# The second layer's memory keys computed in three reduced products instead of one full float32 product

## The chip, the cores and the metric

The kernel runs on one core of one Trainium2 chip. The metric is the device time of one launch in microseconds (us). Names used below: PE is the matrix engine (TensorE), ACT is ScalarE, DVE is VectorE, POOL is GpSimd, SP is the engine that issues most of the weight loads. PSUM is the memory that PE accumulates into.

## The reference, cut to what matters

The whole network is two blocks of two layers each, about 3.1 ms of work; the change touches one product in the second layer of the first block. There the layer norm of the memory, `mem_n` (256 tokens by 1024), is the same for both layers, and each layer makes its own keys and values of it.

```python
def memory_attention(q, mem_n, w_kv):
    k, v = jnp.split(mem_n @ w_kv, 2, axis=-1)      # 256 x 1024 each
    ...
    s = einsum(qh, kh) * (XA_HEAD_DIM ** -0.5)
    o = einsum(softmax(s), vh)

# second layer (i = 1)
u, z, xq = split_cols(h @ w_in, [2048, 3072, 1024])
seq_out = s5(u)                                      # a scan over the 512 tokens
xa = memory_attention(xq, mem_n, xa_w_kv[1])
x = x + (concat([seq_out, xa]) * silu(z)) @ w_out[1]
```

`mem_n @ w_kv[:, :1024]` of this layer is the product that the change is about.

## The kernel before, in words

All activations are held feature-major: 128 features on the partitions, tokens along the free axis. The weights of the whole network are one stream of units of 128 by 1024 float32 (512 KB). SP loads unit after unit into `ring`, which has 4 slots. SP loads unit u when unit u-3 has begun, which the semaphore `begun` counts: PE adds one to it with the first matmul of each unit (for one range of tokens).

A `Gemm` stage multiplies by such a stream. Kind "fm": one output tile of 128 features by all tokens per unit here (8 inner tiles of 128, `KD`). It comes in two forms.

- Plain (`high` is None): PE reads `ring` as float32, one `mm` for each inner tile (line 271). The profile shows two matmul records for each of them.
- In three products (`high` given): weights and activations are each written as a high part rounded to the type fp32r and a low part, the rest. ACT makes the high part of a unit into one of the two slots of `high` (`make_high`, line 363), POOL subtracts it from the unit into `ring_r` (`make_low`, line 354), and PE adds three products: high by high (line 261), high weights by low activations (line 264), low weights by high activations (line 266). Before the first product of a unit PE waits for its low part (`unit_lo`, in `unit`). ACT makes the high part of unit u only when `begun` has reached u, that is when unit u-1 has begun, as there are two slots.

Nearly all large products of the kernel have the second form. `mem_k1`, the memory's keys of the second layer, has the plain one: 8 outputs, 8 units, 256 tokens (`MEMS`), stored by ACT and DVE in turn (`BOTH`, lines 3186 and 3189).

The order of the stages around it is written by hand and is the same on each engine:

1. `u`, the product for the scan's input, 16 outputs. It runs inside the stage `S5Inputs`, which also does, three outputs later (`LAG`), the scan's input blocks 0 to 12: 8 small matmuls each (line 1600) whose tables of 512 KB POOL loads (`load_next`, line 1572). There are two buffers for the tables, so table n+2 is loaded when block n is done (semaphore `added`).
2. `mem_k1`.
3. `S5LastInputs`: blocks 13, 14 and 15, and on POOL the loads of tables 14 and 15.
4. `S5Scan`: 63 steps on DVE alone. It starts when all blocks are copied out.
5. During the scan PE does `xq1`, `z1_xa` (three products each, 512 tokens) and `mem_v1` (plain, 256 tokens).
6. `xa1`, the attention, which waits for the scan and for `mem_v1`. Its scores are line 896.

The numbers of blocks and tables run from 0 to 15. `memn` is the normed memory, 128 by 8 by 256. `z_lo` and `z_hi` are the split parts of another activation; their tiles are free between the first layer's last product (`out0`) and a later stage. `b.norms["parts"]`, `out_hi` and `out_lo` count activations' high and low parts.

Of the kernel before, what the change touches and what calls it, by code (L numbers as in the profile page):

```python
# [16 lines left out]
ALU = mybir.AluOpType  # L17
ACT = mybir.ActivationFunctionType
# [7 lines left out]
KD = D // P  # L26
# [19 lines left out]
MEMS = [(0, N_MEM)]  # L46
# [4 lines left out]
class Chain:  # L51


    def __init__(self, eng, sem):
        self.eng, self.sem, self.n = eng, sem, 0
# [29 lines left out]
class Stage:  # L85
# [5 lines left out]
    def scalar(self, act):  # L91
        pass

    def vector(self, dve):
        pass

    def gpsimd(self, pool):
        pass


class Gemm(Stage):
# [13 lines left out]
    def __init__(self, b, name, kind, x, kt, outs, ranges, store, engines, needs, tiles=None, before=None,  # L115
                 high=None, x_hi=None, after=None, ready=None, slots=None, first_bank=0, late=None):
        self.ready = ready
        self.first_bank = first_bank
        self.after_banks = None
        self.fed = False  # L120
        self.squared_by = None
        self.beside = False
        self.low_elsewhere = False
        self.stored_elsewhere = False
        self.between = None
        self.first_use = {}
        self.flip = 0
        self.late, plain = late, int(late is not None)
        self.then = self.follows = None
        self.after = after  # L130
        self.b, self.name, self.kind, self.x, self.kt = b, name, kind, x, kt
        self.ranges, self.store, self.engines, self.needs = ranges, store, engines, needs
        self.tiles, self.before = tiles, before
        if kind == "fm":
            self.per_out = kt // 8
            self.slots = slots or (4 if len(ranges) == 1 else 2)
            self.body_outs = self.slots
            while self.body_outs * self.per_out % RING:
                self.body_outs += self.slots
            if outs < self.body_outs or outs % self.body_outs:  # L140
                self.body_outs = outs
            self.body_units = self.body_outs * self.per_out
            self.iters = outs // self.body_outs
            self.pars = [o % 2 for o in range(self.body_outs)]
        else:
            self.body_units = kt // 2
            self.body_outs = len(tiles)
            self.tile_banks = list(range(len(tiles)))
            self.slots = len(tiles)
            self.iters = outs  # L150
            self.pars = [i % 2 for i in range(len(tiles))]
        self.unit0 = b.units
        self.full0 = list(b.full)
        self.body_par = [self.pars.count(0), self.pars.count(1)]
        self.peel = min(self.full0) == 0 or self.iters == 1 or before is not None or high is not None
        self.high, self.x_hi, self.split0 = high, x_hi, b.splits - plain
        if high is not None:
            assert self.body_units % 2 == 0 or self.iters == 1, name
            b.splits += self.body_units * self.iters - plain
        b.units += self.body_units * self.iters  # L160
        b.full = [f + self.iters * n for f, n in zip(b.full, self.body_par)]
        self.done = list(b.full)
        if self.iters > 1:
            assert self.body_units % RING == 0, name
# [287 lines left out]
    def gpsimd(self, pool):  # L452
        if self.high is None or self.beside or self.low_elsewhere:
            return

        def body(it):
            for j in range(self.body_units):
                if not (self.late and isinstance(it, int) and it + j == 0):
                    self.make_low(pool, j, it)
        self.loop(pool, body)  # L460

# [794 lines left out]
NB = S5_G // 8  # L1256
# [289 lines left out]
class S5Inputs(Stage):  # L1546
# [7 lines left out]
    def __init__(self, b, m, beside, needs):  # L1554
        self.b, self.m, self.beside, self.needs = b, m, beside, needs
        beside.beside = True
        self.u_in = [b.sem("s5i_u_even"), b.sem("s5i_u_odd")]
        self.block_in = [b.sem("s5i_in_even"), b.sem("s5i_in_odd")]
        self.added = b.sem("s5i_added")
        self.x_kept = b.sem("s5i_x_kept")  # L1560
        self.done = (self.x_kept, NB)

    def load_rows(self, sp, n):

        for k in range(S5_C):
            sp.dma_start(self.m.u[16 * (7 - k):16 * (7 - k) + 16, n * 8:n * 8 + 8],
                         self.b.d_u[n * P:(n + 1) * P].rearrange("(g h) t -> h g t", h=S5_H)[:, :, S5_J * k:S5_J * (k + 1)]
                         ).then_inc(self.u_in[n % 2], 16)
# [5 lines left out]
    def gpsimd(self, pool):  # L1574
        gemm = self.beside
        for s, v in self.needs:
            pool.wait_ge(s, v)
        self.load_table(pool, 0)
        self.load_table(pool, 1)
        gemm.low_unit(pool, 0)  # L1580
        for n in range(NB):
            gemm.low_unit(pool, n + 1)
            if n > self.LAG:
                self.load_next(pool, n - self.LAG - 1)

    def load_next(self, pool, n):

        pool.wait_ge(self.added, n + 1)
        if n + 2 < NB:
            self.load_table(pool, n + 2)  # L1590
# [19 lines left out]
    def scalar(self, act):  # L1610
        gemm = self.beside
        if not gemm.fed:
            gemm.high_unit(act, 0)
        for n in range(NB):
            gemm.high_unit(act, n + 1)
            gemm.out_scalar(act, n)

    def block_vector(self, dve, n):

        b, m = self.b, self.m  # L1620
        dve.wait_ge(self.added, n + 1)
        to = m.state[:, n, 1:S5_J, :]
        b.nc.vector.tensor_copy(to, b.ps[:, 4 + n % 2, :].rearrange("p (g j) -> p j g", g=8)[:, 0:S5_J - 1, :]
                                ).then_inc(self.x_kept, 1)

    def vector(self, dve):
        self.b.chain.link(self.b.nc.vector.memset(self.m.state[:, :, 0, :], 0.0))
        for n in range(NB - self.LAG):
            self.block_vector(dve, n)


class S5LastInputs(Stage):
# [1466 lines left out]
def build(nc, a, out):  # L3099

    with ExitStack() as ctx:
        b = Board(nc, ctx)
# [81 lines left out]
        def copy(which, to, ps, scale=None):  # L3184
            if which == "act":
                return nc.scalar.activation(to, ps, ACT.Copy, scale=1.0 if scale is None else scale)  # L3186
            if scale is not None:
                return nc.vector.tensor_scalar(to, ps, scale, None, ALU.mult)
            return nc.vector.tensor_copy(to, ps)

        def keep(to, scale=None):
            return lambda which, m, parts, o: copy(which, to[:, m, :], parts[0], scale)

        BOTH, A, V = ("act", "dve"), ("act", "act"), ("dve", "dve")
        stages = []
# [60 lines left out]
        memn = lambda k: b.memn[:, k, :]  # L3256
# [3 lines left out]
        def tm_keep(to, width=512):  # L3260
            return lambda which, m, part, o: copy(
                which, to[0:part.shape[0], m[1], bass.ds(m[0] * width, width)], part)
# [29 lines left out]
        class StoreMemory(Stage):  # L3292


            def __init__(self, needs):
                self.needs = needs
# [44 lines left out]
        def add_x(which, m, parts, o):  # L3341
# [15 lines left out]
        s5r = S5Responses(b, m5, g, [gla.done] + tables.done, done(gz0))  # L3357
# [3 lines left out]
        high = b.high  # L3361
        out0_done = [(b.stored[0], g.done[0]), (b.stored[1], g.done[1])]
# [5 lines left out]
                  hi=lambda k: chunked(h_hi(k)[:, 0:L1]), lo=lambda k: chunked(h1_lo(k)), added=True)  # L3368
# [5 lines left out]
        def send_u(act, m, o, par, n):  # L3374
# [7 lines left out]
                           high=high, x_hi=h_hi, after=send_u))  # L3382
        rms.feed(stages[-1])
        gu = stages[-1]
        km1, vm1, xq1 = view(30848, KD, N_MEM), view(28800, 2, D), view(20480, 8, L1)
# [9 lines left out]
        m5.ustage = [memf[:, i * 512:(i + 1) * 512] for i in range(2)]  # L3395
        s5i = S5Inputs(b, m5, gu, tables.done + out0_done)
        stages.append(s5i)
        stages.append(Gemm(b, "mem_k1", "fm", memn, KD, KD, MEMS, keep(km1), BOTH, s5r.done))
        stages.append(S5LastInputs(s5i))
        scan = S5Scan(b, m5, [s5i.done])  # L3400
        stages.append(scan)
# [1 line left out]
        stages.append(Gemm(b, "z1_xa", "fm", h1_lo, KD, D // P, FULL,  # L3403
                           lambda which, m, parts, o: nc.scalar.activation(b.z[:, m + 16, :], parts[0], ACT.Silu), A, [],
                           high=high, x_hi=h_hi))
        stages[-2].lead(stages[-1])
        stages.append(Gemm(b, "mem_v1", "tm", memn, KD, 2, None, tm_keep(vm1), A, [], MEM_TILES))
        g = stages[-1]
# [6 lines left out]
                  high=high, x_hi=h_hi)  # L3415
# [12 lines left out]
                   high=high, x_hi=m5.y_hi)  # L3428
# [15 lines left out]
        def add_x1(which, m, parts, o):  # L3444
# [6 lines left out]
                           x_hi=z_hi, ready=split_z.ready))  # L3451
# [365 lines left out]
```

## Time and profile before

| what | value |
|---|---|
| median of 3 runs | 3115.97 us (3114.11 to 3116.03) |
| the profiled execution | 3121.37 us |
| its span (first to last instruction) | 3119.6 us |
| mean clock granted to PE in it | 0.965 of full |
| PE busy | 2871.5 us (92%) |
| POOL busy | 1067.7 us (34%) |
| ACT busy | 986.1 us (32%) |

Busy shares are means over stages with different limits. The span lacks what lies around the instructions, 1.8 us here. A name such as `arena` is one large buffer that holds many tensors in turn, so a row is placed by its line and time. In the rows "PEclk" is the clock granted to PE, 1.00 for 2.4 GHz and 0.50 for 1.2 GHz. A bracket as [1.10 <-POOL ring_r L354] is the idle time of the engine before this row and what ended it.

### The profile page before, as it was taken

What the parts mean: (1) busy time and instruction counts of PE and PEld (TensorE: products, weight loads), DVE (VectorE), ACT (ScalarE), POOL (GpSimd) and SP (SyncE); (2) the same over time, 40 slices, a digit from 0 to 9 for tenths busy, and PEclk for the clock granted to TensorE, in tenths of its full rate; (3) what the DMA queues carried; (4) which work ended last, traced back from release to release, by engine and by line L of the source; (5) the groups of instructions that cost most, each with busy time, mean ns of one, the idle gap of its engine ahead of it and who ended that gap; (6) DMA issues with size and microseconds to landing.
All of it is one profiled execution on the core that took longest, in us unless ns stands there. A gap on an engine that the chain in (4) does not pass through costs nothing.

```text
span 3119.6 us, 44776 instructions
## 1 busy us (share of the span) xinstructions
PE 2871.5 (92%) x17854; PEld 2346.1 (75%) x17854; DVE 1397.9 (45%) x2227; ACT 986.1 (32%) x1505; POOL 1067.7 (34%) x749
## 2 busy tenths in 40 slices
PE   6988989899899999998989888899998999899997
PEld 4666567677688578786778876799998866668885
DVE  5788364600206611302138574470634345293452
ACT  3222354222312236423225332312124454332221
POOL 0233122344324179444433410144442321234442
PEclk9999999999999999999999998999999998899999
DMA  3898111244572279322222100122222210122222
GB/s 134 260 259 268 69 41 48 78 135 161 154 211 98 95 182 262 104 95 74 88 86 68 36 3 22 61 94 89 88 94 74 78 42 20 54 81 94 95 94 74
DMA packets 130750, 324.85 MB, mean 104 GB/s; under 512 B 54145, under 2 KB 54785, under 8 KB 129809
## 3 DMA queue, kind: packets, MB, share of 16 engines
q1 hardware_dynamic: 96128, 221.90, 21.8%
q0 software_dynamic: 30096, 88.21, 10.2%
q10 hardware_dynamic: 4352, 12.26, 1.0%
q8 instruction: 130, 2.13, 0.3%
q14 instruction: 44, 0.35, 0.0%
HBM read 288.32 MB, written 33.95 MB: 103 GB/s over the span
## 4 chain that ended last, share of the span: by engine, by line
PE 69%; DVE 18%; DMA 4%; ACT 3%; issue 3%; POOL 3%; DVEq 1%; ACTq 0%; SPq 0%; POOLq 0%
PE ps L261 16%; PE ps L264 16%; PE ps L266 16%; PE ps L271 3%; DMA d_pb<-arena 3%; POOL ring_r L354 2%; DVE h L593 1%; PE ps L2829 1%; PE ps L915 1%; PE ps L1769 1%; PE ps L573 1%; PE ps L1510 1%; PE ps L1600 1%; PE ps L2180 1%; PE ps L2804 1%
## 5 line engine op out<-in xcount | busy, mean ns | idle before, releaser
L354 POOL TENSOR_TENSOR ring_r<-ring,high 128x1024 fp32r<-128x1024 f32 x327 | 815.5, 2494 | 1449.9 <-ACT high L363 1449.8
L261 PE MATMUL ps<-h_hi,high 128*128 128x512 f32 (+1 forms) x2104 | 735.1, 358 | 40.3 <-DVE ring_r L354 13.1
L266 PE MATMUL ps<-h_hi,ring_r 128*128 128x512 f32 (+1 forms) x2104 | 661.6, 349 | 0.0
L264 PE MATMUL ps<-h_r,high 128*128 128x512 f32 (+1 forms) x1912 | 643.1, 346 | 0.0
L363 ACT ACTIVATE high<-ring 128x1024 fp32r<-128x1024 f32 x359 | 379.5, 1057 | 822.8 <-PE ps L261 697.4
L261 PEld LDWEIGHTS ps<-h_hi,high 128*128 128x128 f32 x2104 | 399.6, 190 | 117.2 <-issue 48.9
L266 PEld LDWEIGHTS ps<-h_hi,ring_r 128*128 128x128 f32 x2104 | 369.8, 190 | 53.5
L264 PEld LDWEIGHTS ps<-h_r,high 128*128 128x128 f32 x1912 | 364.5, 191 | 41.6 <-issue 1.4
L264 PE MATMUL ps<-f_r,high 128*128 128x264 f32 (+1 forms) x832 | 261.2, 326 | 0.0
L261 PE MATMUL ps<-f_hi,high 128*128 128x264 f32 (+1 forms) x768 | 236.6, 321 | 0.0
L261 PE MATMUL ps<-z_hi,high 128*128 128x512 f32 x488 | 197.9, 405 | 29.7 <-POOL ring_r L354 23.9
L266 PE MATMUL ps<-f_hi,ring_r 128*128 128x264 f32 (+1 forms) x768 | 205.0, 321 | 0.0
L266 PE MATMUL ps<-z_hi,ring_r 128*128 128x512 f32 x488 | 193.2, 396 | 0.0
L264 PEld LDWEIGHTS ps<-f_r,high 128*128 128x128 f32 x832 | 156.7, 188 | 14.4
L3186 ACT ACTIVATE arena<-ps 128x512 f32<-128x512 f32 (+4 forms) x102 | 58.4, 576 | 339.2 <-PE ps L266 250.1
L261 PEld LDWEIGHTS ps<-f_hi,high 128*128 128x128 f32 x768 | 144.4, 188 | 11.4
L264 PE MATMUL ps<-z_lo,high 128*128 128x512 f32 x360 | 145.7, 405 | 0.0
L261 PEld LDWEIGHTS ps<-z_hi,high 128*128 128x128 f32 x488 | 93.4, 191 | 59.6 <-POOL ring_r L354 21.6
L266 PEld LDWEIGHTS ps<-f_hi,ring_r 128*128 128x128 f32 x768 | 127.0, 188 | 11.0
L3619 DVE CAST f_hi<-f x64 | 131.6, 2056 | 7.8
L264 PE MATMUL ps<-z_hi,high 128*128 128x512 f32 x280 | 112.1, 400 | 0.0
L266 PEld LDWEIGHTS ps<-z_hi,ring_r 128*128 128x128 f32 x488 | 93.5, 192 | 22.5
(465 smaller groups left out, 4271.1 us busy)
## 6 DMA issues: line engine op xcount, KB each, us to landing
ring<-in_units SPq DMA_DIRECT2D x402, 512.0 KB, 3.2
d_ca<-arena POOLq DMA_DIRECT2D x16, 640.0 KB, 9.3
arena<-d_ca POOLq DMA_DIRECT2D x16, 640.0 KB, 5.7
arena<-d_q POOLq DMA_DIRECT2D x32, 256.0 KB, 8.3
d_pb<-arena POOLq DMA_DIRECT2D x16, 512.0 KB, 11.4
arena<-d_pb POOLq DMA_DIRECT2D x16, 512.0 KB, 4.1
arena<-d_ca POOLq DMA_DIRECT2D x16, 512.0 KB, 5.0
arena<-d_k POOLq DMA_DIRECT2D x128, 64.0 KB, 4.2
```

Of the source, the lines that this page charges most:

```text
L261: part = mm(acc, hi[:, cols], self.x_hi(k)[:, t0:t0 + tn], start=(k == 0), stop=False)
L264: mm(acc, hi[:, cols], self.x(k)[:, t0:t0 + tn], start=False, stop=False)
L266: ins = mm(acc, w[:, cols], self.x_hi(k)[:, t0:t0 + tn], start=False, stop=(k == self.kt - 1))
L271: ins = mm(acc, w[:, k % 8 * P:(k % 8 + 1) * P], self.x(k)[:, t0:t0 + tn], start=(k == 0), stop=(k == self.kt - 1))
L354: eng.tensor_tensor(b.ring_r[:, slot, :], b.ring[:, slot, :], self.high[:, (j + self.flip) % 2, :], ALU.subtract).then_inc(b.unit_lo, 1)
L363: b.nc.scalar.activation(self.high[:, (j + self.flip) % 2, :], b.ring[:, u % RING, :], ACT.Copy).then_inc(b.unit_hi, 1)
L573: ins = b.nc.tensor.matmul(b.ps[:, bank, 0:tn], b.ones[:, :], b.sq[:, k % 2, t0:t0 + tn], start=(k == 0), stop=(k == self.n - 1))
L593: b.nc.vector.scalar_tensor_tensor(out=self.out(k), in0=self.view(self.x(k)), scalar=self.w(k), in1=self.view(b.inv[:, 0:self.tokens]), op ...
L915: ins = b.nc.tensor.matmul(b.ps[:, 6 + c, :], self.v[:, m, (2 * h + c) * P:(2 * h + c + 1) * P], self.pt[:, h % 2, m, :], start=(m == 0), ...
L1510: ins = mm(b.ps[0:S5_H, 4 + 2 * par + g // 4, g % 4 * P:(g % 4 + 1) * P], m.ca[par][:, g, 144:160], m.ca[par][:, g, 0:P], start=True, stop ...
L3186: return nc.scalar.activation(to, ps, ACT.Copy, scale=1.0 if scale is None else scale)
L3619: nc.vector.tensor_copy(hi, t).then_inc(mlp_parts, 1)
```

## The change

`mem_k1` is given the form in three products. Its activation, the normed memory, is split during the u product by a new class `SplitMemory`, in four quarters of 128 by 512: ACT makes the high parts after outputs 3 to 6 of `u`, POOL the low parts during outputs 4 to 7. They lie in free tiles of `z_lo` (high parts) and `z_hi` (low parts). The first weight unit of `mem_k1` is split ahead, at the end of `S5Inputs` (`follower`); its other seven are split as those of other products are. The first weight unit of `xq1` is split by ACT just before the last store of `mem_k1` (`lead`).

```diff
@@ class Gemm
+        self.low_given = False
@@ Gemm.gpsimd
             for j in range(self.body_units):
-                if not (self.late and isinstance(it, int) and it + j == 0):
+                if not ((self.late or self.low_given) and isinstance(it, int) and it + j == 0):
                     self.make_low(pool, j, it)
@@ S5Inputs.gpsimd
         gemm.low_unit(pool, 0)
         for n in range(NB):
             gemm.low_unit(pool, n + 1)
+            if 4 <= n < 8:
+                self.memory.low(pool, n - 4)
             if n > self.LAG:
                 self.load_next(pool, n - self.LAG - 1)
+        self.follower.low_unit(pool, 0)
@@ S5Inputs.scalar
         for n in range(NB):
             gemm.high_unit(act, n + 1)
+            if n == NB - 1:
+                self.follower.make_high(act, 0, 0)
             gemm.out_scalar(act, n)
+            if 3 <= n < 7:
+                self.memory.high(act, n - 3)
@@
+class SplitMemory:
+
+    def __init__(self, b, free, hi, lo):
+        self.b, self.free, self.hi, self.lo = b, free, hi, lo
+        self.at = b.norms["parts"]
+        b.norms["parts"] += 4
+        self.done = (b.out_lo, self.at + 4)
+
+    def quarter(self, i):
+        return self.b.memn[:, 2 * i:2 * i + 2, :]
+
+    def high(self, act, i):
+        for s, n in self.free if i == 0 else ():
+            act.wait_ge(s, n)
+        self.b.nc.scalar.activation(self.hi[:, 2 * i:2 * i + 2, :], self.quarter(i), ACT.Copy).then_inc(self.b.out_hi, 1)
+
+    def low(self, pool, i):
+        pool.wait_ge(self.b.out_hi, self.at + i + 1)
+        pool.tensor_tensor(self.lo[:, 2 * i:2 * i + 2, :], self.quarter(i), self.hi[:, 2 * i:2 * i + 2, :], ALU.subtract
+                           ).then_inc(self.b.out_lo, 1)
@@
-        stages.append(Gemm(b, "mem_k1", "fm", memn, KD, KD, MEMS, keep(km1), BOTH, s5r.done))
+        by_tile = lambda z: z[:, 20:24, :].rearrange("p a (c t) -> p (a c) t", c=2)
+        mem_hi, mem_lo = by_tile(b.z_lo), by_tile(b.z_hi)
+        s5i.memory = SplitMemory(b, out0_done, mem_hi, mem_lo)
+        gk1 = Gemm(b, "mem_k1", "fm", lambda k: mem_lo[:, k, :], KD, KD, MEMS, keep(km1), BOTH,
+                   s5r.done + [s5i.memory.done], high=high, x_hi=lambda k: mem_hi[:, k, :])
+        s5i.follower, gk1.fed, gk1.given, gk1.low_given = gk1, True, 1, True
+        stages.append(gk1)
...
+        gk1.lead(stages[-2])
```

What the change does to the order is seen on three engines. On PE, at the end of the first unit of `mem_k1` and the start of its second, stood before (two of the eight units, `ring` is the plain float32 unit):

```order
L271 MATMUL ps<-memn,ring 128x256 [waits landed0]
L271 MATMUL ps<-memn,ring 128x256 x7
L271 MATMUL ps<-memn,ring 128x256 [waits landed1,stored_odd]
L271 MATMUL ps<-memn,ring 128x256 x7
L229 REGISTER_ALU
```

and stands now (the last two inner tiles of the first unit, and the first two of the second; `z_lo` is the memory's high part, `z_hi` its low part):

```order
L267 MATMUL ps<-z_lo,ring_r 128x256
L262 MATMUL ps<-z_lo,high 128x256
L265 MATMUL ps<-z_hi,high 128x256
L267 MATMUL ps<-z_lo,ring_r 128x256
L262 MATMUL ps<-z_lo,high 128x256 [waits unit_lo]
L265 MATMUL ps<-z_hi,high 128x256
L267 MATMUL ps<-z_lo,ring_r 128x256
```

A unit had 8 matmul instructions that waited for a load (`landed`); it has 24 now, and the first of them waits for POOL (`unit_lo`).

On ACT, from the last store of `u` to the first of `xq1`, stood before (the two stores are in a loop that runs twice):

```order
L3377 DMA d_u<-arena 128x512 [waits stored_odd]
L187 UNCONDITIONAL_BRANCH
L187 ISA
L3186 ISA [waits filled_even]
L3186 ACTIVATE arena<-ps 128x256
L376 REGISTER_ALU
L3186 ISA [waits filled_even]
L3186 ACTIVATE arena<-ps 128x256
L187 REGISTER_ALU
L187 COMPARE_AND_BRANCH
L363 ACTIVATE high<-ring 128x1024 [waits begun,landed0]
```

and stands now (line 364 was 363):

```order
L3409 DMA d_u<-arena 128x512 [waits stored_odd]
L364 ACTIVATE high<-ring 128x1024 [waits landed1,out_lo,begun,s5r_k_odd,s5r_k_even]
L3218 ACTIVATE arena<-ps 128x256 [waits filled_even]
L364 ACTIVATE high<-ring 128x1024 [waits begun,landed2]
L364 ACTIVATE high<-ring 128x1024 [waits begun,landed3]
L3218 ACTIVATE arena<-ps 128x256 [waits filled_even]
L364 ACTIVATE high<-ring 128x1024 [waits begun,landed0]
L364 ACTIVATE high<-ring 128x1024 [waits begun,landed1]
L3218 ACTIVATE arena<-ps 128x256 [waits filled_even]
```

Seven `make_high` came in between the four stores, and each waits for `begun`.

On POOL, from the last split of `u` (line 354, now 355) to the splits of `xq1`, stood before:

```order
L1572 DMA arena<-d_pb 128x1024 [waits s5i_added]
L354 TENSOR_TENSOR ring_r<-ring,high 128x1024 [waits unit_hi]
L1572 DMA arena<-d_pb 128x1024 [waits s5i_added]
L354 TENSOR_TENSOR ring_r<-ring,high 128x1024 [waits unit_hi]
L1572 DMA arena<-d_pb 128x1024 [waits s5i_added] x4
L354 TENSOR_TENSOR ring_r<-ring,high 128x1024 [waits unit_hi] x16
```

and stands now:

```order
L1574 DMA arena<-d_pb 128x1024 [waits s5i_added]
L355 TENSOR_TENSOR ring_r<-ring,high 128x1024 [waits unit_hi]
L1574 DMA arena<-d_pb 128x1024 [waits s5i_added] x2
L355 TENSOR_TENSOR ring_r<-ring,high 128x1024 [waits unit_hi] x8
L1574 DMA arena<-d_pb 128x1024 [waits s5i_added] x2
L355 TENSOR_TENSOR ring_r<-ring,high 128x1024 [waits unit_hi] x16
```

The eight low parts of `mem_k1` stand ahead of the last two table loads, those of blocks 14 and 15, which followed directly on the loads before them.

## Rows read from the trace of the kernel before

**Rows 1.** The page: the span, and the busy time of the engines.

```profile
span 3119.6 us, 44776 instructions
...
PE 2871.5 (92%) x17854; PEld 2346.1 (75%) x17854; DVE 1397.9 (45%) x2227; ACT 986.1 (32%) x1505; POOL 1067.7 (34%) x749
...
```

**Rows 2.** The chain that ended last, 800 to 1120 us: start, us, what.

```profile
...
912.45 27.68 PE ps L271 x128
940.13 1.75 PE ps L1600 x16
942.16 3.41 DMA arena<-d_pb
945.62 2.44 PE ps L1600 x16
...
1068.93 4.51 PE ps L896 x12
...
```

**Rows 3.** Busy time by stretch (the first line names the columns), mem_k1.

```profile
...
core 0: us, PE busy (x) PEld busy (x) DVE busy (x) ACT busy (x) POOL busy (x), PEclk, DMA share, GB/s
...
912.20:940.00 27.80, 27.80 (x132) 24.49 (x131) 1.96 (x4) 2.59 (x5) 0.53 (x1) 1.00 0.66 198
...
```

**Rows 4.** Timeline of PE, 264-column products: start, us, engine, line.

```profile
...
2096.98 0.29 PE L261 MATMUL ps<-f_hi,high 128*128 128x264 f32 x1
...
2102.82 0.29 PE L261 MATMUL ps<-f_hi,high 128*128 128x264 f32 x1
...
```

**Rows 5.** Timeline, the first split units of the u product.

```profile
...
803.48 2.37 POOL L354 TENSOR_TENSOR ring_r<-ring,high 128x1024 fp32r<-128x1024 f32 x1 [13.50 <-ACT high L363]
...
805.90 0.50 PE L261 MATMUL ps<-h_hi,high 128*128 128x512 f32 x1 [1.10 <-POOL ring_r L354]
...
806.49 1.06 ACT L363 ACTIVATE high<-ring 128x1024 fp32r<-128x1024 f32 x1 [1.06 <-PE ps L261]
...
```

**Rows 6.** Timeline of POOL alone, from the same place on.

```profile
...
807.63 2.41 POOL L354 TENSOR_TENSOR ring_r<-ring,high 128x1024 fp32r<-128x1024 f32 x1 [1.78 <-ACT high L363]
...
855.36 2.40 POOL L354 TENSOR_TENSOR ring_r<-ring,high 128x1024 fp32r<-128x1024 f32 x1 [4.40 <-ACT high L363]
...
912.75 0.53 POOL L1572 DMA_DIRECT2D arena<-d_pb  x1 [6.78 <-PE ps L1600]
942.16 0.53 POOL L1572 DMA_DIRECT2D arena<-d_pb  x1 [28.88 <-PE ps L1600]
...
```

**Rows 7.** Instructions on f_hi: ns min/median/max of one, forms.

```profile
...
L261 PE MATMUL ps<-f_hi,high x768: 281/288/397, 2097.0 to 3097.5; 128*128 128x264 f32 x128, 128*128 128x512 f32 x64
...
```

**Rows 8.** Timeline of ACT alone: a 128x512 copy, the u product, mem_v1's last.

```profile
...
791.20 0.63 ACT L554 ACTIVATE h_hi<-h 128x512 fp32r<-128x512 f32 x1 [3.65 <-DVE h L593]
...
854.22 1.06 ACT L363 ACTIVATE high<-ring 128x1024 fp32r<-128x1024 f32 x1 [1.48 <-PE ps L261]
...
1067.03 0.60 ACT L3186 ACTIVATE arena<-ps 128x512 f32 x1 [1.11 <-PE ps L294]
...
```

**Rows 9.** Groups of POOL by shape: xcount | busy, mean ns | idle.

```profile
...
L713 POOL TENSOR_TENSOR x<-x,inv 128x512 f32<-128x512 f32 x8 | 10.2, 1272 | 0.7
...
```

**Rows 10.** Line 1572, the table loads: landing times.

```profile
...
DMA to landing us min/median/max: 3.4/4.1/6.2
```

**Rows 11.** Engines by stretch: PE's gaps and the clock.

```profile
...
1102.00:1110.00 8.00, 6.56 (x19) 3.31 (x19) 2.25 (x5) 0.55 (x2) 3.87 (x8) 0.79 0.29 66
803.00:807.00 4.00, 2.90 (x13) 2.05 (x12) 0.73 (x2) 1.50 (x3) 2.37 (x1) 1.00 0.17 64
...
```

**Rows 12.** Engines by stretch, a part of the second block's first stage.

```profile
...
1760.00:1764.00 4.00, 2.38 (x59) 1.92 (x54) 1.54 (x4) 0.48 (x2) 3.80 (x8) 1.00 0.00 0
...
```

**Rows 13.** Engines by stretch, one microsecond each.

```profile
...
946.00:947.00 1.00, 1.00 (x11) 1.00 (x11) 0.00 (x0) 0.00 (x0) 0.00 (x0) 1.00 0.08 16
947.00:948.00 1.00, 1.00 (x7) 1.00 (x7) 0.00 (x0) 0.00 (x0) 0.00 (x0) 0.52 0.00 0
...
951.00:952.00 1.00, 1.00 (x6) 0.83 (x5) 0.58 (x2) 0.00 (x0) 1.00 (x1) 1.00 0.42 168
...
```

More of the change, by code:

```diff
@@ L1561, in __init__ @@
         self.done = (self.x_kept, NB)
+        self.memory, self.follower = None, None
     def load_rows(self, sp, n):
```

## The prediction

> **What bounds the kernel now.** I read the page first: PE works for 2871.5 of 3119.6 us [rows 1], so the question for a change to one product is whether PE's time there is on the chain. The chain of waits around the place says yes [rows 2]: it runs through `mem_k1` without a break for 27.68 us, then through one of the three last input blocks (1.75 us), the load of table 15 (3.41 us), the last block (2.44 us), then the scan on DVE, and comes back to PE at 1068.93 us with the attention's scores. The scan can't start before the last block, and the last block not before `mem_k1` is done: every microsecond that `mem_k1` gains or loses moves the scan, and with it the rest of the kernel. The stretch itself [rows 3] shows PE busy for all of it at a clock of 1.00, ACT for 2.6 us, POOL for 0.5 us: PE alone bounds `mem_k1` now, at 27.68 / 8 = 3.46 us for a unit.
>
> **The change, PE's part.** A unit becomes 24 matmuls of 256 columns. The trace has none of these, but it has the same three lines with 264 columns in the second block [rows 4]: an inner tile is 6 matmuls there, two halves of the tokens by three products, and the two rows begin inner tiles that are 8 apart (line 261 comes 16 times from the first up to the second); that is 48 matmuls in 5.84 us, 0.122 us each. At 2.4 GHz 264 columns are 0.110 us; with the remaining 0.012 us, 256 columns take 0.118 us, and 24 of them 2.84 us. If nothing else counted, `mem_k1` would take 8 x 2.84 = 22.7 us, a gain of 5.0 us.
>
> The Trainium skill (FP8 and Floating Point Precision, TensorE Precision Notes) says that true FP32 takes four passes through the array; three products are then 3/4 of the columns, 20.8 us by that alone. The trace agrees with the four passes: 27.68 us for 64 products is 0.43 us each, four times 256 columns at 2.4 GHz.
>
> **The change, the wait that it adds.** PE may not begin a unit before its low part is there, POOL makes that after ACT's high part, and ACT starts the high part only when the unit before has begun. So a unit's period can't be shorter than this round. With 512 columns a unit of 24 x (0.118 + 0.107) = 5.4 us hides it; a unit of 2.84 us does not. Each link stands in the trace, best at the start of the u product, where PE did wait for it [rows 5, 6]:
> - from PE's first matmul to ACT's start: 805.90 to 806.49 us, 0.59 us, of which the matmul's own record is 0.50. The 264-column record is 0.28 us at the median and 0.40 at most [rows 7]; after a wait I take 0.39, so 0.48 us in all.
> - from ACT's start to POOL's: 806.49 to 807.63 us, 1.14 us.
> - POOL's subtraction: 2.40 us.
> - from POOL's end to PE's next first matmul: 803.48 + 2.37 to 805.90, 0.05 us.
>
> The sum is 4.07 us. The first unit is split ahead, so seven such periods stand between its start and that of the last unit, and the last one runs its 2.84 us: 28.5 + 2.84 = 31.3 us, with 0.1 us for the first matmul after a wait 31.4. Against 27.68 us that is 3.75 us more. With POOL at 2.37 us, as in [rows 5], a round is 4.04 us, the sum 31.1, the loss 3.4; with the full 0.59 us of the first link it is 4.18 us, the sum 32.3, the loss 4.6. I take the middle value, since a 256-column matmul is nearer to the 264-column one. POOL alone is busy 2.40 of 4.07 us, ACT 1.06: it is the serial round and not the load of either that binds.
>
> **The change, the parts that I cost at nothing.**
> - ACT's four copies of 128 by 512: such a copy takes 0.63 us, and before every high part in the u product ACT was free for 1.48 us, in which it only issues one DMA [rows 8]. Without that cover the four would cost 2.5 us.
> - POOL's four subtractions of half the size: 1.20 us by half of 2.40, 1.27 us by the nearest row [rows 9]; POOL idles 4.40 us before each split there [rows 6]. Queued behind each is a table load, which is needed two blocks later, and a block comes every 2.40 + 0.53 + 4.40 = 7.3 us. Uncovered they would cost 5.1 us.
> - The first unit's split, made while PE still runs the last output of `u`, and `xq1`'s first, made by ACT before the last store: both hidden, the one by the 5.4 us of that output, the other by the last unit and the three input blocks.
> - The stores, (2.59 - 1.06) / 4 = 0.38 us each on ACT [rows 3]: they fall into ACT's and DVE's idle time in a round.
> - The weight loads: the ring was fed at 3.46 us for a unit with the DMA engines 0.66 busy [rows 3]; it is asked for a unit every 4.07 us now.
> - POOL's queue: the load of table 14 was issued at 912.75 us, at the start of `mem_k1` [rows 6], and stands now behind all eight low parts, thus at the start of the last unit. Block 14 comes 2.84 + 1.75 = 4.6 us after that; the landing takes 3.4 to 6.2 us, 4.1 at the median [rows 10]. Even at 6.2 block 14 ends 7.95 us after the issue, and block 15 can't start before 4.6 + 0.28 + 3.41 = 8.3, as its own load waits for block 13 (0.28 us from that block's end at 940.13 + 1.75 to the issue at 942.16). So nothing.
> - PE's own way to the attention also moves by the same time: its last store before it ends at 1067.63 us [rows 8], 1.3 us ahead of the scan's end.
>
> **The sum.** +3.75 us, nothing against it: `mem_k1` in the profile 31.4 us, the span 3119.6 + 3.8 = 3123.4 us. The profiled execution took 3121.37 us, 5.4 us above the median of the runs, so the sum is put on the median: 3115.97 + 3.8 = 3119.8 us. A difference below 0.2% (6.2 us) is about what a measurement of this kernel can't tell from none.
>
> **The rivals.**
> - *The clock falls in `mem_k1`.* PE would idle 1.2 us in every 4.07. For: the clock fell to 0.52 at 947 us, after the light blocks and a wait of 2 us, and was back at 951 [rows 13]; it was 0.79 over a stretch of the attention with PE busy for 6.56 of 8 us [rows 11]. Against: at 803 to 807 us, with the same gap of 1.1 us and PE busy 2.90 of 4 us, it stayed at 1.00 [rows 11], and so it did at 2.38 of 4 us of small products [rows 12]. At half the clock a unit takes at most 5.7 us, 1.6 more than a round. One stretch of 4 us costs 1.6 us, and from two units on, with the 3.8, it is 3123; from the second or third on it passes 6.2 us; all eight units would give 3133. Chance 0.10. It is the case that ends clearly slower.
> - *The round doesn't bind*, because ACT makes the high parts earlier than I read: then the 5.0 us are gained, 3111.0 us. This ends on the faster side of the forecast, still under 0.2%. Against it: ACT's wait for PE's line 261 stands in the bracket of each high part [rows 5, 8]. It decides as soon as a round is shorter than 3.46 us. Chance 0.05.
> - *The low clock comes earlier after it.* PE enters the three blocks less busy than before, and a block took 1.75 us at full clock and 2.44 with the clock falling [rows 2]: two more slow blocks and a slow last unit are up to 1.4 + 2.8 us, 3121 to 3124. Chance 0.07.
> - *The loss is taken up later*, or the change does nothing to the end: something in the scan or the attention would have to wait for a thing that doesn't move; the attention has only the 1.3 us named. 3115 to 3117 us. Chance 0.04.
>
> The Trainium skill (TensorE: Matmul & The Clock Gate, "A second HAM failure mode: psum-queue depth-cycling") tells of a kernel in which short idles between groups of matmuls made the clock swing between its levels. By that rule the first rival is the likely one, and its time stands there. This trace doesn't bear it out at gaps of this length [rows 11, 12].
>
> **How the numbers follow.** The forecast has 0.74, its own range 3119 to 3121. The range of 8 in 10 reaches down over the case of the loss taken up, 3115.5, and up over the slow blocks and the mildest clock case, 3125.5; outside it stay the gain (0.05), most of the clock case (0.08), and some of the rest. Slower by over 0.2% is the clock case and a little of the slow blocks, 0.11; faster by over 0.2% needs more than PE's whole saving, 0.01; the rest, 0.88, is within 0.2%.
>
> **What would show it.** In the profile after: `mem_k1` from its first row to the next line 1600 row 31.4 us; PE's line 261 waiting seven times for POOL's `ring_r`, 1.1 to 1.3 us each, where before there was no idle time; POOL's rows there 4.07 us apart, each with a bracket of some 1.7 us for ACT's high part; PE's busy time in it near 24 us; the last block's wait for its table still near 2 us; the scan of the same length, 4 us later. Wrong would be: no such waits (then the gain), waits of over 1.5 us, a clock under 1.00 before 945 us, or a wait of PE for table 14.

## The result and the profile after

| what | before | after |
|---|---|---|
| median, 9 runs each | 3115.08 us (3113.26 to 3121.26) | 3121.76 us (3116.93 to 3126.90) |
| ratio, 95% interval | 1 | 1.0022 (1.0012 to 1.0031) |
| the same two in a later comparison, 29 and 11 runs | 3115.91 us | 3117.94 us, ratio 1.0008 (0.9998 to 1.0018) |
| span of the profiled execution | 3119.6 us | 3116.1 us |

The change makes the kernel slower, by 0.1 to 0.2%: 6.7 us in the first comparison and 2.0 us in the second, whose interval just takes in no change. The profile shows +4.5 us at the place of the change (below), a ratio of 1.0014, and that lies in both intervals. The span of the one profiled execution is shorter than that of before. So the whole span of a single execution says nothing here; the place has to be read.

The chain of waits of the changed kernel, its first round and then from 930 us on, to set beside [rows 2] (start, us, what; lines 262, 355, 364 and 1605 were 261, 354, 363 and 1600):

```profile
...
909.74 1.73 PE ps L1605 x16
911.47 0.19 PE ps L262
911.76 1.07 ACT high L364
912.90 2.38 POOL ring_r L355
915.32 0.40 PE ps L262
...
931.66 0.37 PE ps L262
932.12 1.07 ACT high L364
933.25 2.39 POOL ring_r L355
935.78 0.37 PE ps L262
936.23 1.07 ACT high L364
937.37 2.39 POOL ring_r L355
939.90 0.36 PE ps L262
942.98 1.75 PE ps L1605 x16
945.02 3.49 DMA arena<-d_pb
948.54 3.02 PE ps L1605 x16
951.59 0.70 DVE arena L1632
...
```

Where the chain was one piece of PE, 27.68 us, it now goes round three engines: the first matmul of a unit, ACT's high part, POOL's low part, the next unit's first matmul. Only the last unit (939.90 to 942.98) is PE's own time. Block 12, before `mem_k1`, ends at 911.47 us, and block 13 begins at 942.98: 31.5 us, 3.8 more than before. To the end of the last block it is 40.1 us, 35.6 before: 4.5 more.

The waits of PE in that stretch (us in total, times, longest):

```profile
PE ps L262 <- POOL ring_r L355: 7.0, 7, 1.0
```

Seven waits of 1.0 us, where there were none. The same as busy time by stretch, to set beside [rows 3]:

```profile
core 0: us, PE busy (x) PEld busy (x) DVE busy (x) ACT busy (x) POOL busy (x), PEclk, DMA share, GB/s
911.28:942.80 31.52, 24.55 (x194) 23.25 (x194) 1.95 (x4) 10.02 (x12) 17.13 (x8) 1.00 0.51 156
948.50:951.60 3.10, 3.06 (x17) 3.06 (x18) 0.01 (x1) 0.00 (x0) 0.00 (x0) 0.63 0.02 5
```

PE's busy time fell from 27.80 to 24.55 us and the stretch grew from 27.8 to 31.5: PE is idle for 7.0 us. The clock stayed at 1.00 all through. The second row is the last input block, at a clock of 0.63: it took 3.02 us, 2.44 before.

Some rounds in POOL's timeline, beside [rows 6]:

```profile
...
916.94 2.37 POOL L355 TENSOR_TENSOR ring_r<-ring,high 128x1024 fp32r<-128x1024 f32 x1 [1.67 <-ACT high L364]
920.98 2.38 POOL L355 TENSOR_TENSOR ring_r<-ring,high 128x1024 fp32r<-128x1024 f32 x1 [1.67 <-ACT high L364]
925.03 2.37 POOL L355 TENSOR_TENSOR ring_r<-ring,high 128x1024 fp32r<-128x1024 f32 x1 [1.67 <-ACT high L364]
929.14 2.38 POOL L355 TENSOR_TENSOR ring_r<-ring,high 128x1024 fp32r<-128x1024 f32 x1 [1.74 <-ACT high L364]
...
```

POOL starts every 4.04 us at first, and every 4.11 us from the fifth unit on; it waits for ACT for 1.7 us each time, so POOL's load by itself isn't the bound.

### The profile page after: what moved, and what is told of

It is laid out like the page before. It is cut to its first block, busy times and chain, and to the rows that moved or that the text cites. A ratio compares the mean times of both kernels' runs of the same rounds, so it can differ in the third digit from the quotient of the medians.

```text
span 3116.1 us, 44903 instructions
## 1 busy us (share of the span) xinstructions
PE 2859.6 (92%) x17918; PEld 2336.8 (75%) x17918; DVE 1399.7 (45%) x2227; ACT 997.8 (32%) x1517; POOL 1098.2 (35%) x761
## 4 chain that ended last, share of the span: by engine, by line
PE 69%; DVE 17%; ACT 4%; DMA 4%; POOL 3%; issue 3%; DVEq 1%; ACTq 0%; SPq 0%; POOLq 0%
PE ps L262 17%; PE ps L265 16%; PE ps L267 16%; DMA d_pb<-arena 3%; POOL ring_r L355 2%; PE ps L272 2%; DVE h L594 1%; PE ps L1801 1%; PE ps L916 1%; PE ps L1511 1%; ACT high L364 1%; PE ps L2861 1%; PE ps L574 1%; PE ps L1605 1%; PE ps L2212 1%
## 5 line engine op out<-in xcount | busy, mean ns | idle before, releaser
L355 POOL TENSOR_TENSOR ring_r<-ring,high 128x1024 fp32r<-128x1024 f32 x335 | 841.4, 2512 | 1461.7 <-ACT high L364 1461.6
L364 ACT ACTIVATE high<-ring 128x1024 fp32r<-128x1024 f32 x367 | 388.0, 1057 | 830.5 <-PE ps L262 706.5
L262 PE MATMUL ps<-z_hi,high 128*128 128x512 f32 x488 | 197.3, 404 | 19.0 <-POOL ring_r L355 13.2
L3218 ACT ACTIVATE arena<-ps 128x512 f32<-128x512 f32 (+3 forms) x102 | 58.4, 575 | 324.5 <-PE ps L267 256.7
L265 PE MATMUL ps<-z_hi,high 128*128 128x512 f32 (+1 forms) x344 | 130.1, 378 | 0.0
```

The lines of the kernel that those rows point to most:

```text
L262: part = mm(acc, hi[:, cols], self.x_hi(k)[:, t0:t0 + tn], start=(k == 0), stop=False)
L265: mm(acc, hi[:, cols], self.x(k)[:, t0:t0 + tn], start=False, stop=False)
L355: eng.tensor_tensor(b.ring_r[:, slot, :], b.ring[:, slot, :], self.high[:, (j + self.flip) % 2, :], ALU.subtract).then_inc(b.unit_lo, 1)
L364: b.nc.scalar.activation(self.high[:, (j + self.flip) % 2, :], b.ring[:, u % RING, :], ACT.Copy).then_inc(b.unit_hi, 1)
```

## The experiments

Each was timed against the kernel before on the same chip. The first four ran on one chip, the three at the end on another. Runs of one kernel lie 20 us and more apart there, in the kernel before too (35 runs, 3103.6 to 3125.2 us), so the intervals reach 3 to 5 us to each side, and each profile's place is read as well.

**The low parts on DVE.** Edit, on top of the changed kernel:

```diff
+        gk1.low_elsewhere = gk1.stored_elsewhere = True
+
+        class KeysOnVector(Stage):
+
+            def vector(self, dve):
+                gk1.low_unit(dve, 1)
+                for o in range(1, KD, 2):
+                    gk1.low_unit(dve, o + 1)
+                    it, at = divmod(o, gk1.body_outs)
+                    par, n = gk1.count(at, it)
+                    dve.wait_ge(b.filled[par], n)
+                    gk1.store("dve", o, gk1.bank(at), at).then_inc(b.stored[par], 1)
+                    gk1.low_unit(dve, o + 2)
+
         stages.append(gk1)
+        stages.append(KeysOnVector())
...
```

> The changed kernel, with the low parts of mem_k1's units 1 to 7 made by DVE (1.22 us each) in place of POOL (2.38 us); the table loads of blocks 14 and 15 stand on POOL where they stood before the change. Theory A, the serial round from a unit's begin through ACT and the subtracting engine bounds mem_k1: the round shrinks from 4.07 to about 2.9 us, PE's own 2.84 us; mem_k1 takes 23 us in the profile, 4.5 less than before and 8.4 less than the changed kernel; time 3110.5 to 3111.5. Theory B, the loss comes from something else (the spacing of 256-column matmuls, the clock, the ring's loads): mem_k1 stays above 27 us. A part of A may be lost to the ring: its first units come behind the rows of u in SP's queue, up to 2 us.

Measured: 3111.2 us median of 11 against 3113.8 of 35, ratio 0.9988 (0.9976 to 1.0), so the gain over the kernel before is at the edge of what can be told from none. In the profile `mem_k1` takes 24.1 us, where 23 were expected. Busy time of that stretch:

```profile
912.10:936.25 24.15, 23.55 (x194) 23.16 (x194) 10.45 (x11) 9.80 (x12) 0.57 (x1) 1.00 0.79 225
```

PE is busy for 23.55 of 24.15 us. The subtraction by another engine takes 7.4 us off the changed kernel's stretch, with PE's own work the same (the last two table loads stand earlier on POOL too, which the next experiment leaves out). What is left of waiting is one gap of 0.59 us, PE's for DVE at 924.4 us, and before it ACT had waited for the ring (first row; the longer wait of the second row didn't reach PE):

```profile
921.95 1.06 ACT L364 ACTIVATE high<-ring 128x1024 fp32r<-128x1024 f32 x1 [0.57 <-DMA ring<-in_units]
925.04 1.06 ACT L364 ACTIVATE high<-ring 128x1024 fp32r<-128x1024 f32 x1 [2.02 <-DMA ring<-in_units]
...
```

So theory A holds, and the next bound seems to be the ring: SP's queue has the rows of `u` between its loads. The kernel with SP's rows later tests that.

**A third slot for the high parts.** POOL still subtracts; ACT makes the high parts one unit earlier (slots `high` 0, `sq`, `high` 1 in turn), and its stores stand behind them.

```diff
+        if self.third is None:
+            return self.high[:, (j + self.flip) % 2, :]
+        return (self.high[:, 0, :], self.third, self.high[:, 1, :])[j % 3]
...
-            act.wait_ge(b.begun, u + it * self.body_units)
+            act.wait_ge(b.begun, u + it * self.body_units - (self.third is not None and it + j > 0))
...
+        gk1.third = b.sq_r[:, :, :].rearrange("p a t -> p (a t)")[:, 0:UNIT]
...
+            gk1.high_unit(act, 1)
+            gk1.high_unit(act, 2)
+            for o in range(KD):
+                if o == KD - 1:
+                    gk1.then.make_high(act, 0, 0)
+                gk1.out_scalar(act, o)
+                gk1.high_unit(act, o + 3)
```

> The changed kernel, with a third slot for the high parts of mem_k1's units (in sq), so that ACT and POOL work up to two units ahead; POOL still subtracts. Theory A: the round of about 4.1 us has two units' time (5.7 us) to run in, so PE doesn't wait and mem_k1 takes about 23 us; POOL is busy 2.38 of 2.87 us. Time 3110.5 to 3111.5. If POOL's speed itself were the bound and not the round, it would be the same 23 us, at 2.45 us for a unit; if the cause is not on ACT's and POOL's side at all, 31 us as now.

Measured: 3112.8 us against 3113.8, ratio 0.9994 (0.9980 to 1.0008); `mem_k1` 24.9 us. Its three waits of PE, and the wait of ACT for the ring that stands before the last and longest of them:

```profile
...
915.54 0.39 PE L263 MATMUL ps<-z_lo,sq_r 128*128 128x256 f32 x1 [0.15 <-POOL ring_r L362]
...
924.74 0.36 PE L263 MATMUL ps<-z_lo,sq_r 128*128 128x256 f32 x1 [0.41 <-POOL ring_r L362]
...
928.61 0.36 PE L263 MATMUL ps<-z_lo,high 128*128 128x256 f32 x1 [0.79 <-POOL ring_r L362]
...
```

```profile
924.94 1.06 ACT L371 ACTIVATE high<-ring 128x1024 fp32r<-128x1024 f32 x1 [2.54 <-DMA ring<-in_units]
...
```

POOL does the same seven subtractions in `mem_k1` as in the changed kernel (16.7 us of work), and `mem_k1` is 6.6 us shorter. What bound it was the order in time, one unit after the other, and not POOL's speed. The remaining 1.4 us of waiting come mostly from the ring again: ACT had waited for it before the waits of 0.41 and 0.79 us. The expected 23 us were not reached, since I had not counted SP's queue. The total's gain can't be told from none. In this profile the clock fell 0.3 us into the last block, which took 3.43 us.

**More work on PE, no idle time.** The kernel before with nine products more after `mem_k1`:

```diff
+        class MoreWork(Stage):
...
+            def tensor(self, pe):
+                for i in range(9):
+                    nc.tensor.matmul(b.ps[:, 6, 0:N_MEM], b.memn[:, i % KD, 0:P], memn(i % KD), start=True, stop=True)
+        stages.append(MoreWork())
```

> The kernel before, with nine more float32 products of 128 by 128 by 256 after mem_k1 into an unused bank (nothing of the output changes): 9 x 0.43 = 3.9 us of PE work, with no idle time of PE and no work for ACT and POOL. The changed kernel lost 6.7 us at the median, of which the stretch from mem_k1 to the scan shows 4.5 us in the profile. Theory A, a shift of this place goes to the end one to one: +3.9 us, 3119. Theory C, the rest of the loss (2.2 us) comes from PE having idled in mem_k1 and the clock after it: this kernel loses only 3.9 and its runs lie as near to each other as those before. Theory D, any shift of the later program against the clock's changes costs this and widens the scatter: 3120 to 3122, runs 5 to 10 us apart.

Measured: 3116.6 us (12 runs) against 3113.8, ratio 1.0009 (0.9992 to 1.0026). In the chain the nine products are 3.88 us:

```profile
...
914.57 27.68 PE ps L271 x128
942.26 3.88 PE ps L3404 x18
946.14 1.75 PE ps L1600 x16
948.17 3.53 DMA arena<-d_pb
951.74 2.87 PE ps L1600 x16
...
```

From the start of `mem_k1` to the end of the last block it is 40.0 us, before 35.6 and with the change 40.1; the attention's first scores come 161.0 us after the start, before 156.5 and with the change 161.0. From the end of the last block to those scores it is 120.9 us in each of the nine profiles, wherever `mem_k1` took 23.3 or 31.5 us. So a loss or a gain here goes on whole to the attention, whether PE works or idles. The last block was slow (2.87 us) without any idle time in `mem_k1`, so its slow clock isn't put down to those gaps. The total, +2.7 us with an interval from -2.5 to +8.1, agrees with +3.9 and doesn't tell theory A from D. Nor does the scatter: the runs lie 27.7 us apart (3106.6 to 3134.3), one of them far above the others, but those of the kernel before lie 21.5 us apart, so "5 to 10 us apart" could not have been a sign of theory D.

**The splitting of the memory alone.** `mem_k1` is plain again; the eight copies and subtractions remain, and nothing reads them.

```diff
-        self.follower.low_unit(pool, 0)
...
-            if n == NB - 1:
-                self.follower.make_high(act, 0, 0)
...
-        gk1 = Gemm(b, "mem_k1", "fm", lambda k: mem_lo[:, k, :], KD, KD, MEMS, keep(km1), BOTH,
-                   s5r.done + [s5i.memory.done], high=high, x_hi=lambda k: mem_hi[:, k, :])
-        s5i.follower, gk1.fed, gk1.given, gk1.low_given = gk1, True, 1, True
+        gk1 = Gemm(b, "mem_k1", "fm", memn, KD, KD, MEMS, keep(km1), BOTH, s5r.done + [s5i.memory.done])
...
-        gk1.lead(stages[-2])
```

> The changed kernel, with mem_k1's plain float32 product put back: only the memory's four high copies on ACT and four subtractions on POOL during the u product remain (nobody reads them). If these are hidden, as the prediction had it: the time of the kernel before, 3115 plus or minus 1, and the period of the u product's blocks stays 7.33 us. If they delay a table load or a split: up to 7.6 us more (4 x 0.63 and 4 x 1.27).

Measured: 3113.9 us against 3113.8, ratio 0.9999 (0.9986 to 1.0011), and the period in POOL's timeline is still 7.33 us:

```profile
838.25 2.40 POOL L355 TENSOR_TENSOR ring_r<-ring,high 128x1024 fp32r<-128x1024 f32 x1 [3.15 <-ACT high L364]
840.62 1.28 POOL L1657 TENSOR_TENSOR z_hi<-memn,z_lo 128x512 fp32r<-128x512 f32 x1
841.86 0.57 POOL L1574 DMA_DIRECT2D arena<-d_pb  x1
845.58 2.40 POOL L355 TENSOR_TENSOR ring_r<-ring,high 128x1024 fp32r<-128x1024 f32 x1 [3.15 <-ACT high L364]
...
```

The subtraction of 1.28 us came out of idle time that was 4.40 us and is 3.15 now. From PE's wait for the second weight unit of `u` to the start of `mem_k1` it is 106.56 us (803.43 to 909.99), and 106.55 before (805.90 to 912.45). So the splitting costs nothing at the place; the loss is in the product.

**The changed kernel again, the version with DVE again, and with SP's rows later.** The third is the DVE version with this edit:

```diff
...
-                    if 0 <= u - first_row < NB:
-                        rows(u - first_row)
+                    n = u - first_row
+                    if 0 <= n < NB - 2 or late is None and 0 <= n < NB:
+                        rows(n)
+                    if late is not None and n in late:
+                        rows(late[n])
...
-            _, end = beside(u_at, u_rows)
+            _, end = beside(u_at, u_rows, {16: 14, 18: 15})
```

> The changed kernel, once more, against the kernel before. Theory A, all of the loss is the round in mem_k1 and the slow last block (31.5 in place of 27.7 us, and 3.0 in place of 2.4): +4.4 us, and the 6.7 us of the first comparison are 2 us of scatter. Theory C, idle gaps of PE make later parts slower too: +6 to +7 again. The place itself in the profile: mem_k1 31.5 us again, give or take 0.1, while the last block and the attention may differ by where the clock's changes fall.

Measured: 3117.9 us (11 runs) against 3115.9 (29), ratio 1.0008 (0.9998 to 1.0018). `mem_k1` 31.5 us again, its waits 0.94 to 1.04 us again, the last block 2.62 us. Theory A's 1.0014 lies in the interval, theory C's 6 us (1.0019) is just outside it.

> The kernel in which DVE makes the low parts, once more, on the same chip as the changed kernel. mem_k1 24.1 us again; between it and the changed kernel 7.4 us in mem_k1 plus up to 1 us of the last block at the low clock: 7 to 9 us at the medians, if the round is the cause. A difference under 4 us would speak against it.

Measured: 3112.1 us (12 runs), ratio 0.9989 (0.9978 to 1.0); `mem_k1` 24.2 us. Between the medians of this and the changed kernel on one chip are 5.9 us, against 7.3 us in `mem_k1`: less than the 7 to 9 expected, above the 4 that would have spoken against the round.

> DVE makes the low parts, as in the first experiment, and SP issues the last two groups of u's rows (8 loads each, for the input blocks 14 and 15) two and three ring loads later. If the last microsecond that PE waits in that experiment's mem_k1 (0.59 us at 924.4, and lesser ones) comes from ring loads that queue behind these rows, ACT never waits for the ring now, and mem_k1 takes 23.0 to 23.3 us in place of 24.1; time 1 us less than that one, 3110. If the ring's loads are slow by themselves (shared bandwidth), it stays at 24.

Measured: 3112.6 us (12 runs), ratio 0.9992 (0.9980 to 1.0005). The expected microsecond can't be seen in the time (3110 was expected), but it is in the place: `mem_k1` takes 23.3 us, PE waits no more, and ACT's high parts wait for PE alone. So the ring's loads were late by their place in SP's queue, and not slow by themselves. Busy time of the stretch, and a piece of SP's queue:

```profile
913.20:936.50 23.30, 23.30 (x195) 23.14 (x194) 10.53 (x11) 9.57 (x12) 0.57 (x1) 1.00 0.75 231
```

```profile
913.52 6.12 SPq L3771 DMA_DIRECT2D ring<-in_units  x3
919.68 3.74 SPq L1568 DMA_DIRECT2D arena<-d_u  x8
923.47 2.03 SPq L3771 DMA_DIRECT2D ring<-in_units  x2
...
```

All kernels at the place of the change, in us from their chains (start of `mem_k1` to the end of the last block holds block 13, the wait for table 15 and what lies between too):

| kernel | `mem_k1` | last block | start of `mem_k1` to end of last block |
|---|---|---|---|
| before | 27.7 | 2.44 | 35.6 |
| after | 31.5 | 3.02 | 40.1 |
| after, again | 31.5 | 2.62 | 39.7 |
| low parts on DVE | 24.1 | 2.67 | 32.4 |
| the same, again | 24.2 | 2.56 | 32.3 |
| third slot | 24.9 | 3.43 | 33.9 |
| more work on PE | 27.7 + 3.9 | 2.87 | 40.0 |
| splitting alone | 27.7 | 2.32 | 35.5 |
| DVE, rows later | 23.3 | 2.01 | 30.9 |

## Why the prediction was right

- *PE alone bounds the place, and it hands its time on whole*: right. The attention's scores moved by 4.5 us against the start of `mem_k1`, and by the same in the kernel with more work on PE.
- *256 columns at 0.118 us, a unit at 2.84 us*: right. In the kernel with SP's rows later, where PE never waits, 23.3 us are 2.91 for a unit, and an inner tile of three matmuls takes 0.355 us, 0.118 each. The other 0.07 us is the first matmul of a unit: it has 0.14 to 0.27 us in that run's chain, where the others have 0.12.
- *The round of 4.07 us, seven times*: right as a mechanism. From unit start to unit start the seven rounds took 3.85, 4.04, 4.05, 4.14, 4.11, 4.12 and 4.12 us, 4.06 at the mean. That the mean fits to 0.01 us is partly luck, as the first round is shorter than taken and the last four are longer. In the first round PE had not waited, its first matmul has 0.19 us in the chain, and the first link was 0.29 us (911.47 to 911.76). After a wait it was 0.48 us as taken (915.32 to 915.80) or 0.45, ACT to POOL 1.14, POOL 2.37, and POOL to PE 0.05. For outputs 4 to 7 this last link was 0.14 us: there PE's first matmul waits for a free bank as well, which I had not counted; that this is the reason wasn't tested. The third slot and DVE each remove the round in another way, and the waits go.
- *`mem_k1` at 31.4 us, +3.75*: 31.5 and +3.8. The last unit took 3.08 us, where 2.94 was taken, as its first matmul after the wait has 0.36 us. The sums for the two other values of the round have slips of 0.1 us: with the same 0.1 us for that matmul, 4.04 us give 31.2 (+3.5), and 4.18 give 32.2 (+4.5).
- *Waits of PE of 1.1 to 1.3 us, PE busy for near 24 us*: the waits were 0.94 to 1.04 us, below the forecast, and the busy time 24.55 us. The forecast set a round of 4.07 against a unit of 2.84 us, but after a wait PE's first matmul has 0.36 to 0.39 us in place of 0.118, so a unit is some 3.1 us of busy time. The round's length doesn't change by this, since it begins with that matmul.
- *The splitting of the memory at nothing*: right, shown by the kernel that has only this.
- *POOL's queue with the load of table 14 behind the low parts, nothing*: right. The load was issued at 939.69 us, and PE waited for none but table 15, 2.05 us; with DVE the load is where it was before, and that wait is as long.
- *The clock doesn't fall in `mem_k1`*: right. It is 1.00 over the stretch with PE busy for 24.55 of 31.52 us. The Trainium skill (TensorE: Matmul & The Clock Gate, "A second HAM failure mode: psum-queue depth-cycling") describes a kernel whose clock swung at short idles between groups of matmuls. This case, with idles of 1.0 us in every 4.1, does not show it.
- *The sum of +3.8 us* was too low for the place by 0.7 us in the first profile and 0.2 in the second (40.1 and 39.7 us against 35.6): the last input block took 3.02 and 2.62 us where it was 2.44, and the load of table 15 took 0.05 to 0.08 us longer. I had this as a rival ("the low clock comes earlier after it") and left it out of the sum. In the profile it is there, smaller than that rival's price, and in the kernel with more work on PE too, which has no idle time; and its length goes with how early the clock falls in it. It is not shown that the change causes that.
- *The predicted 3119.8 us* stands between the two comparisons, 3121.8 and 3117.9, and both lie outside the forecast's own narrow range of 3119 to 3121, so the total confirms the order of size and no more. What the first has above the place's 4.5 us, 2.2 us, wasn't in the second, and no run names a cause; it is within the scatter of the runs. What confirms the forecast is the place.

## What to carry to other kernels

When a product is split into cheaper ones and other engines prepare each unit, compare PE's new time for a unit with the full round of the preparation, from the event that allows it to the event that PE waits for, and not with the busy time of the preparing engines. Here ACT and POOL together worked for 3.4 us of a round of 4.1, one after the other, the wider products hid it, and the narrow one (2.9 us) did not. One more slot, or a faster engine for one link, turned the loss at this place (4.5 and 4.0 us) into a gain of 1.7 to 3.3 us; the next bound was where the loads stood in their queue, and moving them made the gain 4.7 us.

## What the runs showed of the hardware

- The same subtraction of 128 by 1024 into fp32r took 2.38 us on POOL and 1.23 us on DVE.
- The same work of the attention took 42.3 us at a mean clock of 0.92 (before), 41.2 at 0.96 (after), and 39.5 at 1.00 (splitting alone). In the last of them nothing had changed in this stretch; the rows are, in that order:

```profile
1068.90:1111.20 42.30, 38.46 (x148) 24.33 (x148) 18.19 (x56) 14.65 (x50) 10.29 (x18) 0.92 0.20 50
```

```profile
1072.40:1113.60 41.20, 37.09 (x148) 23.23 (x149) 18.17 (x56) 15.56 (x50) 10.28 (x19) 0.96 0.20 52
```

```profile
1066.30:1105.80 39.50, 35.37 (x148) 22.61 (x148) 18.18 (x56) 14.86 (x50) 10.28 (x18) 1.00 0.21 54
```

So the clock makes 2.8 us of difference in a single stage from one execution to the next, over half of the whole effect of this change. This is why the place is read here and not the span.
- In each of the nine profiles the clock was 1.00 through `mem_k1` and the wait for table 15, and fell to 0.50 in the block behind it, 0.3 to 1.9 us after its start. A fall followed in all nine on an idle time of PE of 2.0 to 2.1 us after light blocks; the seven idle times of 1.0 us between dense units, in two profiles, had no fall.
